# Seven block products in place of eight in the second feed-forward product of 11 chunks

## What is computed

```
hf = rmsnorm(x, g_ffn)
x = x + jnp.square(jax.nn.relu(hf @ w_ff1)) @ w_ff2     # w_ff1 1024 x 4096, w_ff2 4096 x 1024
```

## Time and profile before

| | us |
|---|---|
| median of 3 runs (2118.06 to 2118.43) | 2118.18 |
| the profiled execution | 2113.45 |
| its span in the trace | 2111.5 |
| TensorE busy, matmuls | 2061.7 |
| VectorE busy | 1071.4 |
| ScalarE busy | 446.9 |
| GpSimd busy | 214.6 |

### The profile page before, as it was taken

How to read it: one execution, slowest core, us unless ns; L and a number is a source line. 1 busy time by engine, 2 the same in 40 slices (tenths; PEclk the granted TensorE clock), 3 DMA queues, 4 the chain that set the end, 5 groups by cost and what they waited for, 6 DMA issues and landing times.

```text
span 2111.5 us, 29081 instructions
## 1 busy us (share of the span) xinstructions
PE 2061.7 (98%) x12888; PEld 2029.7 (96%) x12888; DVE 1071.4 (51%) x1423; ACT 446.9 (21%) x560; POOL 214.6 (10%) x294
## 2 busy tenths in 40 slices
PE   8999899999999999999999999999999999999997
PEld 7888899999999999999999889999999999999997
DVE  8988464455453535253558725633343434343346
ACT  6232441111010111111332234301111111111112
POOL 2353120000000000000110331100000000000003
PEclk9999999999999999999999999999999999999999
DMA  5455111111211112123242641111111111111112
GB/s 178 136 149 161 55 55 51 51 41 41 92 61 52 61 42 70 42 62 132 94 134 71 188 123 41 41 51 40 51 40 41 50 41 50 41 50 41 40 51 85
DMA packets 62493, 152.77 MB, mean 72 GB/s; under 512 B 8576, under 2 KB 21408, under 8 KB 61984
## 3 DMA queue, kind: packets, MB, share of 16 engines
q1 hardware_dynamic: 49552, 112.76, 17.0%
q0 software_dynamic: 9072, 24.65, 4.2%
q10 hardware_dynamic: 3744, 13.50, 1.6%
HBM read 123.36 MB, written 27.53 MB: 71 GB/s over the span
## 4 chain that ended last, share of the span: by engine, by line
PE 95%; DVE 2%; ACT 1%; DMA 1%; issue 1%; POOL 0%; ACTq 0%; DVEq 0%; POOLq 0%
PE tile L509 89%; PE tile L837 2%; PE small L721 1%; PE small L715 1%; PE small L623 1%; PE small L597 0%; DVE pool_s L1224 0%; POOL y_a L1859 0%; DMA y_a<-ya_dram 0%; ACT w_high L871 0%; PE small L565 0%; DMA ya_dram<-u_blocks 0%; PE small L538 0%; ACT u_blocks L1105 0%; DVE rms L1744 0%
## 5 line engine op out<-in xcount | busy, mean ns | idle before, releaser
L1562 DVE TENSOR_TENSOR x<-tile,x 128x816 f32<-128x816 f32 (+1 forms) x304 | 205.6, 718 | 486.9 <-PE tile L509 476.7
L509 PE MATMUL tile<-h_high,w_high 128*128 128x408 f32 (+1 forms) x1920 | 426.0, 330 | 10.4 <-DVE w_low L1237 10.4
L509 PE MATMUL tile<-h_low,w_high 128*128 128x408 f32 (+1 forms) x1920 | 422.4, 328 | 0.0
L509 PE MATMUL tile<-h_high,w_low 128*128 128x408 f32 (+1 forms) x1920 | 422.3, 328 | 0.0
L509 PEld LDWEIGHTS tile<-h_high,w_high 128*128 128x128 f32 x1920 | 320.6, 188 | 13.7 <-issue 12.3
L509 PEld LDWEIGHTS tile<-h_low,w_high 128*128 128x128 f32 x1920 | 320.0, 188 | 1.0
L509 PEld LDWEIGHTS tile<-h_high,w_low 128*128 128x128 f32 x1920 | 319.8, 188 | 1.0
L509 PE MATMUL tile<-hidden_high,w_high 128*128 128x408 f32 (+1 forms) x1440 | 317.8, 329 | 0.7
L509 PE MATMUL tile<-hidden_low,w_high 128*128 128x408 f32 (+1 forms) x1440 | 316.4, 328 | 0.0
L509 PE MATMUL tile<-hidden_high,w_low 128*128 128x408 f32 (+1 forms) x1440 | 316.4, 328 | 0.0
L871 ACT ACTIVATE w_high<-w_raw 128x1024 fp32r<-128x1024 f32 x162 | 170.4, 1052 | 672.9 <-PE tile L509 665.6
(11 more groups left out here) (212 smaller groups left out, 1684.3 us busy)
## 6 DMA issues: line engine op xcount, KB each, us to landing
w_raw<-w_blocks SPq DMA_DIRECT2D x164, 512.0 KB, 3.6
x<-x_t ACTq DMA_DIRECT2D x8, 544.0 KB, 10.6
u_blocks<-ua_dram SPq DMA_DIRECT2D x64, 68.0 KB, 2.8
ya_dram<-u_blocks ACTq DMA_DIRECT2D x8, 544.0 KB, 3.0
y_a<-ya_dram POOLq DMA_DIRECT2D x64, 68.0 KB, 2.7
x_kept<-x ACTq DMA_DIRECT2D x8, 544.0 KB, 2.7
cy_dram<-y_quarter POOLq DMA_DIRECT2D x16, 256.0 KB, 2.9
carry_weights<-cy_dram POOLq DMA_DIRECT2D x8, 512.0 KB, 5.3
```

The costliest lines, as they stand in the source:

```text
L509: mm = pe.matmul(ps[tile][:, c, 0:(b - a) * J], lhs, xt[:, k, a * J:b * J], start=(first and n == 0), stop=(last and n == 2))
L1562: ins = v.tensor_tensor(xt, pt_, xt, ALU.add)
```

## The change

In chunks 3 to 6 of layer 0 and 0 to 6 of layer 1 (`SEVEN`) the second product is made by a scheme with seven block products for a 2 x 2 block product. The hidden 512 are split in two times 256 (with j the 128 within each), the tokens into two halves of 544, the outputs of one turn q (512 of them) into row blocks 0 and 1. From the squared relus seven operands of 256 x 544 are formed (four of them differences), from each q's four quarters of weights (w11, w12, w21, w22) seven operands (four of them sums or differences). A stage n of 28 = 2 turns x 7 products x 2 pairs is 12 matmuls of 272 columns. Products 2, 3, 4 and 6 do not clear their PSUM banks but add to what an earlier stage left, and each stage is read by VectorE into x: what stands in PSUM at that point is the sum that this part of x wants. The eight banks, now one tensor `sums`, are used in four pairs.

A group is the weights of two stages, 128 x 512. Its high part is a ScalarE copy; for the low part ScalarE writes minus the high part into `w_low`, and GpSimd issues a DMA that adds the source onto it. The groups go through a ring of four halves of `w_high` and `w_low`. SyncE fetches quarters by runs of 128 elements, 16 DMAs of 128 KB per chunk, into `w_raw` and the new `w_raw_more`. The squares move from VectorE to ScalarE in these chunks. The preparation of layer 1's state weights moves to chunks 0 (tables, rotations) and 1 and 2 (two quarters each), as `w_raw_more` and the operands take its space. Numbers of blocks and tiles come from tables now. The core of the diff (blank added lines left out):

```diff
+HALF = T // 2
+PART = HALF // 2
...
+SEVEN = (tuple(range(3, 7)), tuple(range(7)))
+N_READ, N_GROUP, N_SUM = 28, 14, 8
...
+        seven_hi = at("seven_high", G, [P, 7, 2, HALF], F32R)
+        seven_lo = at("seven_low", G + 14 * HALF, [P, 7, 2, HALF], F32R)
+        extra = at("w_raw_more", G + 28 * HALF, [P, 4, 512])
...
+        def ring(w_part, g):
+            return w_part[:, g % 4 // 2, 512 * (g % 2):512 * (g % 2) + 512]
...
+        def group_source(q, i):
+            return (part_of_raw(0), part_of_raw(1), part_of_raw(2), part_of_raw(3),
+                    extra[:, 0, :], extra[:, 2, :], extra[:, 1 + 2 * q, :])[i]
...
+        def operand_at(i):
+            src, h = ((tr, 0), (tr, 0), (tr, 0), (ts, 1), (tr, 1), (ts, 0), (tr, 0))[i]
+            return src[:, h * HALF:(h + 1) * HALF]
...
+        def banks(n):
+            first = (0, 6, 2, 4)[n % 4]
+            return acc[:, first:first + 2, 0:PART]
...
+        def group_drained(eng, g):
+            eng.wait_ge(group_hi, g + 1)
+            eng.wait_ge(group_lo[g % 4], 16 * (g // 4 + 1))
...
+            def fetch_quarter(l, cc, q, a, k, dst):
+                m = l * NB + B_FF + 16 * (cc // 2) + KD + KA * q
+                cols = slice(512 * (cc % 2), 512 * (cc % 2) + 512)
+                src = (w_blocks[m:m + KA, :, cols].rearrange("(i a) p (j k n) -> p a k j i n", a=2, k=2, n=P))[:, a, k]
+                to = dst.rearrange("p (i j n) -> p j i n", i=2, n=P)
+                for j in range(2):
+                    sp.dma_start(to[:, j], src[:, j]).then_inc(quarter_in[2 * a + k], 16)
+            def fetch_quarters(l, cc):
+                z = FF_SEVEN[l][cc]
+                g, n = N_GROUP * z, N_SUM * z
+                sp.wait_ge(wlo_made, ff_block(l, cc, 2) + 1)
+                fetch_quarter(l, cc, 0, 0, 0, part_of_raw(0))
+                fetch_quarter(l, cc, 0, 1, 0, part_of_raw(1))
+                if z == 0:
+                    prepared(sp)
+                else:
+                    sp.wait_ge(quarter_summed, n)
+                    group_drained(sp, g - 8)
+                fetch_quarter(l, cc, 0, 1, 1, extra[:, 1, :])
+                if z:
+                    group_drained(sp, g - 2)
+                fetch_quarter(l, cc, 0, 0, 1, extra[:, 2, :])
+                sp.wait_ge(quarter_summed, n + 3)
+                if z:
+                    group_drained(sp, g - 1)
+                fetch_quarter(l, cc, 1, 1, 1, extra[:, 3, :])
+                group_drained(sp, g)
+                fetch_quarter(l, cc, 1, 0, 0, part_of_raw(0))
+                group_drained(sp, g + 1)
+                fetch_quarter(l, cc, 1, 1, 0, part_of_raw(1))
+                sp.wait_ge(quarter_summed, n + 4)
+                group_drained(sp, g + 5)
+                fetch_quarter(l, cc, 1, 0, 1, extra[:, 2, :])
...
+            def seven_products(l, cc):
+                z = FF_SEVEN[l][cc]
+                for n in range(N_READ):
+                    q, i, pair = n // 14, n % 14 // 2, n % 2
+                    g = N_GROUP * z + n // 2
+                    if pair == 0:
+                        group_drained(pe, g)
+                    if n in (0, 2, 3):
+                        pe.wait_ge(tile_free, ff1_tile(l, cc, 2 if n == 0 else 3) + 1 + 2)
+                    elif n == 1:
+                        pe.wait_ge(small_free, SM[(("kernel", 1, 3, 1), ("sum", 3, 2))[l]] + 1 + 2)
+                    else:
+                        pe.wait_ge(seven_read, N_READ * z + n - 3)
+                    out = banks(n)
+                    for j in range(2):
+                        if n < 14 and pair == 0:
+                            pe.wait_ge(operand_lo, N_GROUP * z + 7 * j + i + 1)
+                        cols = slice(2 * P * pair + P * j, 2 * P * pair + P * j + P)
+                        for t, (wt, xt) in enumerate(((whi, seven_hi), (whi, seven_lo), (wlo, seven_hi))):
+                            lhs = ring(wt, g)[:, cols]
+                            for h in range(2):
+                                mm = pe.matmul(out[:, h, :], lhs, xt[:, i, j, h * PART:(h + 1) * PART],
+                                               start=(i in (0, 1, 5) and j == 0 and t == 0), stop=(j == 1 and t == 2),
+                                               skip_group_check=i in (2, 3, 4, 6))
...
+            def group_ready(l, cc, n):
+                z = FF_SEVEN[l][cc]
+                q, i = divmod(n, 7)
+                if n < 4:
+                    act.wait_ge(tile_done, ff1_tile(l, cc, 2 + n // 2) + 1)
+                else:
+                    act.wait_ge(seven_done, N_READ * z + 2 * (n - 4) + 2)
+                if i in (0, 5, 6):
+                    act.wait_ge(quarter_in[(0, 1, 3)[(0, 5, 6).index(i)]], 32 * (2 * z + q + 1))
+                else:
+                    act.wait_ge(quarter_summed, N_SUM * z + 4 * q + {4: 1, 1: 2, 2: 3, 3: 4}[i])
+            def minus_high(l, cc, n):
+                group_ready(l, cc, n)
+                act.activation(ring(wlo, N_GROUP * FF_SEVEN[l][cc] + n), group_source(*divmod(n, 7)), ACT.Copy,
+                               scale=-1.0).then_inc(group_minus, 1)
+            def high(l, cc, n):
+                act.activation(ring(whi, N_GROUP * FF_SEVEN[l][cc] + n), group_source(*divmod(n, 7)),
+                               ACT.Copy).then_inc(group_hi, 1)
...
+            def seven_hidden(l, cc):
+                z = FF_SEVEN[l][cc]
+                def squares(m):
+                    act.wait_ge(tile_free, ff1_tile(l, cc, m) + 1 + 2)
+                    for h in (1, 0):
+                        part = (tr, ts)[m % 2][:, h * HALF:(h + 1) * HALF]
+                        act.activation(part, part, ACT.Square).then_inc(half_squared, 1)
...
+                for j in range(2):
+                    squares(2 * j)
+                    operand(j, 0)
+                    if j == 0:
+                        ahead(ff_block(l, cc, 2), ff1_tile(l, cc, 0))
+                    operand(j, 1)
+                    if j:
+                        for n in range(2):
+                            minus_high(l, cc, n)
+                            high(l, cc, n)
+                        minus_high(l, cc, 2)
+                        high(l, cc, 2)
+                    squares(2 * j + 1)
+                    if j == 0:
+                        ahead(ff_block(l, cc, 3), ff1_tile(l, cc, 1))
+                        for i in range(2, 7):
+                            operand(j, i)
+                minus_high(l, cc, 3)
+                operand(1, 2)
+                minus_high(l, cc, 4)
+                operand(1, 3)
+                high(l, cc, 3)
+                operand(1, 4)
+                high(l, cc, 4)
+                operand(1, 5)
+                operand(1, 6)
+                for n in range(5, N_GROUP):
+                    minus_high(l, cc, n)
+                    high(l, cc, n)
+                for n in range(2):
+                    act.wait_ge(seven_done, N_READ * z + 24 + 4 * n)
+                    split_hi(ff_block(l, cc + 1, n))
...
+            def seven_chunk(l, cc):
...
+                def low(j, i):
+                    v.wait_ge(operand_hi, N_GROUP * z + 7 * j + i + 1)
+                    v.tensor_tensor(seven_lo[:, i, j, :], operand_at(i), f32(seven_hi[:, i, j, :]),
+                                    ALU.subtract).then_inc(operand_lo, 1)
...
+                def weight_sums(q, which):
+                    w11, w12, w21, w22 = part_of_raw(0), extra[:, 2, :], part_of_raw(1), extra[:, 1 + 2 * q, :]
+                    if which == 0:
+                        if q:
+                            group_drained(v, N_GROUP * z + 4)
+                        quarter_sum(q, 0, extra[:, 0, :], w11, w21, ALU.subtract, (0, 2))
+                        quarter_sum(q, 1, w21, w21, w22, ALU.add, (3,))
+                        if q:
+                            group_drained(v, N_GROUP * z + 2)
+                        v.wait_ge(quarter_summed, N_SUM * z + 4 * q + 2)
+                        quarter_sum(q, 2, part_of_raw(2), w21, w11, ALU.subtract, ())
+                    else:
+                        if q:
+                            group_drained(v, N_GROUP * z + 3)
+                        v.wait_ge(quarter_summed, N_SUM * z + 4 * q + 3)
+                        quarter_sum(q, 3, part_of_raw(3), w12, part_of_raw(2), ALU.subtract, (1,))
+                def read(n):
+                    q, i, pair = n // 14, n % 14 // 2, n % 2
+                    row, h = ((0, 0), (1, 1), (0, 1), (0, 1), (1, 1), (0, 0), (1, 0))[i]
+                    v.wait_ge(seven_done, N_READ * z + n + 1)
+                    since = (None, None, None, 2, 6, 10, None)[i]
+                    if since:
+                        v.wait_ge(seven_read, N_READ * z + n - since + 1)
+                    to = in_parts(x[:, KA * q + 2 * pair + row, h * HALF:(h + 1) * HALF])
+                    v.tensor_tensor(to, banks(n), to, ALU.add).then_inc(seven_read, 1)
```

(58 more changed lines are left out.)

233 lines of the change are left out of this document (164 added, 69 removed).

## The result

| | before | after |
|---|---|---|
| median of 4 runs each, us | 2118.12 (2115.33 to 2118.43) | 2054.86 (2052.47 to 2055.19) |
| the profiled execution | 2113.45 | 2054.69 |
| its span | 2111.5 | 2052.9 |

The account below looks back on a forecast made before the run. TensorE's matmul columns were taken as the bound. 63.8 saved less 3.3, 1.3 and 0.7 gave 58.5 us: profiled execution 2055.0, median 2059.7, range 2048 to 2090, with 2048 to 2072 for the main forecast (0.60).

Parts of the forecast that it names:

- The price of a matmul: Second product: 336 matmuls of 272 columns at 125 ns, 42.0 us, 5.8 less per chunk, 63.8 us in 11 chunks.
- The lows of the weights: Accumulating DMAs for 14 groups per chunk: no wait before the first stage or third group up to 5.4 us landing time.
- L: Time of an accumulating DMA from issue to landing, taken as 4.3 us with ends 2.9 and 7.4.
- VectorE's order: VectorE's reads, operands and sums in a changed chunk: worst backlog at stage 10, which wants read 6, slack 1.8 us.
- The charge of 0.3 per chunk for handoffs: Allowance in each changed chunk for handoffs placed too early: 0.3 us per chunk, 3.3 us in all.
- Layer 1's first chunk: VectorE, held by three reciprocals, reaches its first relu late, so the first stage waits: 1.3 us once.
- The rotation piece: Chunk 0's second product: the first 5.4 us piece on VectorE stands between reads of tiles 0 and 1: 0.7 us lost.
- The offset: Median of runs taken to lie 4.7 us above the profiled execution, turning 2055.0 into 2059.7.
- Slow lows: Rival: L between 5.4 and 8, each changed chunk waits once before its first stage; 2083 at 7.4; chance 0.16.
- the ring: Rival: over L = 8.25 the four slots of low parts make every group late, up to 2262; chance 0.13.
- Dear matmuls: Rival: the second product's 272-column matmuls cost 133 ns, so the gain is 29 us: 2089; chance 0.08.

Follow-up runs that it names:

- eight: Changed kernel with product 0 of each turn made twice, 384 matmuls per second product in place of 336: 2120.20 us, ratio 1.0018 to the kernel before.
- no_first: Changed kernel with layer 1's first chunk left as before, so 10 changed chunks: 2056.46 us, ratio 0.9723 to the kernel before.
- lag2: Changed kernel with ScalarE writing minus the high part of groups 5 to 13 two stages (3.0 us) later: 2073.17 us, ratio 0.9799 to the kernel before.
- lows_vector: Changed kernel with VectorE making the weights' low parts by subtraction, without minus copy or accumulating DMA: 2062.77 us, ratio 0.9750 to the kernel before.
- dve_squares: Changed kernel with the squares of the changed chunks back on VectorE: 2053.48 us, ratio 0.9707 to the kernel before.
- early_rot: Changed kernel with the first group's minus high part written earlier and the first rotation piece one VectorE read later: 2052.35 us, ratio 0.9701 to the kernel before.
- prep_only: Changed kernel with no changed chunk, only layer 1's preparation moved and the new PSUM and number tables: 2116.32 us, ratio 1.0000 to the kernel before.
- dose_free: Changed kernel with a 256 KB copy, in turn to eight places, issued ahead of each accumulating DMA: 2069.53 us, ratio 0.9785 to the kernel before.
- lag4: Changed kernel with ScalarE writing minus the high part of groups 5 to 13 four stages (6.0 us) later: 2175.22 us, ratio 1.0282 to the kernel before.
- lows_vector_late: lows_vector with VectorE's three weight sums of the second turn behind read 7 in place of read 5: 2052.87 us, ratio 0.9701 to the kernel before.

## Why the prediction was right, and where it was off

**What bounds the kernel** held: TensorE's columns. eight and no_first show it from both sides.

**The price of a matmul.** 125 ns taken, 125.3 measured; 5.8 per chunk against 5.89, 63.8 against 64.8 in all. The formula of the Trainium skill (TensorE: Matmul & The Clock Gate, Back-to-back issue gap), which that section calls the gap of an isolated matmul, would have given 115.8 ns; here 125.3 was measured. The upper bound of 133 ns, worked out from the 408-column rows, was no better a guide: eight shows that the same columns cost 48.10 us per second product as four matmuls of 272 for each 1088, and 95.66-47.68 = 47.98 as three.

**The lows of the weights.** L was taken as 4.3, one number. It is 3.5 in the median and 3.2 to 7.0 in the spread. The tolerances were fairly placed (5.4 worked out and 4.74 measured at the first and third group; 7.8 and 7.9 in the ring, for which the rival's sum used 8.25). But "no stall until L > 5.4" was too safe, by 0.7 us, and only the ring's 7.9 covers the slow landings; lag2 shows what happens when they aren't covered. That they fall on the tenth group, where the lead is long, and not on the first or third, was forecast by nothing in the prediction: it is luck.

**VectorE's order.** Slack at stage 10 was worked out as 1.8. Read 6 ends near 742.3 and the stage starts at 743.7, 1.4 later, of which lows_vector shows 1.15 to be usable. dve_squares and lows_vector bracket it: a read 6 that begins 1.03 us later is free, one 2.06 later is not.

**The charge of 0.3 per chunk for handoffs** is the term that was wrong. It was 0 in ten of the 11 chunks, and the eleventh's losses are counted below: 3.3 of the 4.8 us by which the forecast of the gain was short. I had derived slack of 1.1 us or more at every place and then charged for lateness all the same.

**Once per program.** Layer 1's first chunk: 1.3 forecast, 1.47 measured. The reason given (VectorE late by the reciprocals, the first group's DMA with it) accounts for 0.71 idle and 42.34-42.09 = 0.25 of restart. L was smaller than taken, but the DMA was issued only 1361.69-1359.02 = 2.67 us before the first product ended, where 3.0 were worked out. The other 0.5 us had no term: the same late VectorE also made a low part of the first product's weights late, in the list of TensorE's waits from 1320 to 1365 us

```profile
PE sums L647 <- DVE w_low L1497: 0.3, 1, 0.3
```

and the 144 matmuls after it took 24.06 us where 23.84 is usual. early_rot keeps this wait. That the total of 1.3 came so near is in part chance. The rotation piece: 0.7 forecast, 0.63 measured. With them the chain gives 64.8-1.47-0.63 = 62.7; measured 63.3, the rest is under what runs can tell.

**The offset.** I added the 4.7 us by which the profiled execution of before lay under its median. After, the profiled execution lies at the median; its granted clock in layer 0's mixer was lower than before (0.83 against 0.91 from 205 to 225 us, 0.95 against 1.00 from 225 to 260). The spans differ by 58.6, the medians by 63.3, and the latter fits the chain. So it is chance that the profiled execution, worked out as 2055.0, came at 2054.69: it saved 4 us more in the chunks than forecast and lost 3.4 in the mixers, 2.6 of them before layer 0's feed-forward part. prep_only, with the same code there and the median of before, speaks against these 2.6 being the change's.

**The rivals.** Slow lows and the ring did not come: L stayed under its limits but for the 0.71 above. Both mechanisms exist, though. dose_free is the first, 17 us, and lag4 the second, slower than before by 59.7. Dear matmuls (133 ns) are ruled out by 125.3 in ten chunks.

**The best version** measured is early_rot or lows_vector_late, which the runs don't separate from each other or from the change. Both together weren't tried.

## What to carry to other kernels

Where one engine does 98% of the span, an eighth less of its work is an eighth less time in that part, if each feeder meets its date. So work out for each feeder not its share but its dates: the worst backlog on the engine, the lead of each transfer, the period of whoever issues. A lead has to cover the slowest landing, not the median one. And look whether the same work would fit on another engine whose times scatter less, a few instructions later in its order: here moving three operations by two reads was worth 10 us.

## What the runs showed of the hardware that was not expected

- A GpSimd DMA that adds 256 KB of SBUF onto SBUF takes 0.87 us to issue (a plain one 0.77) and 3.2 to 7.0 us to land, as against 2.9 for the same bytes written to DRAM. In each of the 11 chunks the one issued just before SyncE's fetch of the next chunk's weights took 5.6 to 7.0.
- A wait of TensorE costs more than its idle time: 0.25 to 0.34 us more for each, and about 1.5 more where the granted clock fell behind it (in lag2 after 1.94 us idle, not after 1.47 or 1.76).
- With the columns the same, a third more matmuls (384 for 288) cost 0.13 us per second product.
- The granted clock in the mixer differs between executions: the 189 matmuls before layer 0's feed-forward part took 31.75 us before, 33.30 in the changed kernel's profile, and 31.77 and 33.28 in early_rot and lows_vector, which are the same there. It is no effect of the change, and makes single profiles differ by 1.5 us there.
